# A hybrid mLSTM and windowed-attention layer on one core: an opening in smaller blocks, another order of the split products, and projection waits placed ahead of the attention matmuls

## The reference: what is computed

```
mod = silu(c) @ w_ada + b_ada                        # shift, scale, gate; for c and for c_ctx
u = rmsnorm(x, norm_pre_w) * (1 + scale) + shift
aq, ak, av, az, mq, mk, mv, mo, mz, mg, ga, gb = split(u @ w_in)     # w_in is 2048 x 11792
y_b = windowed_attention(rope(aq), rope(ak), av, cached context k, v, sink) * silu(az)
y_a = head_norm(mlstm forward + backward) * sigmoid(mo) * silu(mz)   # 4 heads x 256
merged = sigmoid(ga) * (y_a @ w_proj_a) + sigmoid(gb) * (y_b @ w_proj_b)
out = x + gate * rmsnorm(merged @ w_out, norm_post_w)
```

## Time and profile before

| | |
|---|---|
| median of 3 runs | 2206.77 us (2204.64 to 2209.23) |
| the profiled execution | 2208.73 us, its span 2206.9 us |
| TensorE (PE) matmuls busy | 2114.0 us, 96% of the span |
| VectorE (DVE) busy | 868.7 us, 39% |
| ScalarE (ACT) busy | 643.5 us, 29% |
| GpSimd (POOL) busy | 109.3 us, 5% |
| moved by DMA | 274.07 MB, 124 GB/s on average |
| granted TensorE clock, mean | 0.983 of full |

### The profile page before, as it was taken

How to read it: one execution, slowest core, us unless ns; L and a number is a source line. 1 busy time by engine, 2 the same in 40 slices (tenths; PEclk the granted TensorE clock), 3 DMA queues, 4 the chain that set the end, 5 groups by cost and what they waited for, 6 DMA issues and landing times.

```text
span 2206.9 us, 33978 instructions
## 1 busy us (share of the span) xinstructions
PE 2114.0 (96%) x13450; PEld 1968.9 (89%) x13450; DVE 868.7 (39%) x1674; ACT 643.5 (29%) x1046; POOL 109.3 (5%) x188
## 2 busy tenths in 40 slices
PE   2889999989999999999999989999999999999997
PEld 0559999989999999999999979999999999997885
DVE  4774755532223222323322224343434533352223
ACT  4764112133223232322322221313131422231221
POOL 2001000000000000000000000000000100000001
PEclk7999999999999999999999989999999999999998
DMA  6874755552234224222422243525252644323223
GB/s 243 276 239 124 210 170 174 157 152 83 76 86 117 76 83 120 86 76 76 120 78 81 85 117 81 160 79 152 86 154 81 199 124 120 118 88 124 77 77 143
DMA packets 295170, 274.07 MB, mean 124 GB/s; under 512 B 17920, under 2 KB 243960, under 8 KB 292640
## 3 DMA queue, kind: packets, MB, share of 16 engines
q1 hardware_dynamic: 282416, 218.21, 35.1%
q0 software_dynamic: 12656, 54.40, 6.7%
HBM read 232.65 MB, written 39.92 MB: 124 GB/s over the span
## 4 chain that ended last, share of the span: by engine, by line
PE 91%; DVE 3%; DMA 2%; ACT 1%; issue 1%; SPq 1%; DVEq 0%; POOL 0%; ACTq 0%; POOLq 0%
PE bank L1414 66%; PE bank L1629 10%; PE bank L1503 2%; PE bank L1329 2%; PE bank L1385 2%; PE bank L1368 2%; PE bank L1552 2%; PE bank L1543 1%; PE bank L1554 1%; PE bank L1476 1%; DMA Y<-in_x_prompt_dram 1%; DMA RAW<-in_w_in_dram 1%; DVE WL L875 0%; DVE XL L875 0%; DVE Y L917 0%
## 5 line engine op out<-in xcount | busy, mean ns | idle before, releaser
L1414 PE MATMUL bank<-XH,WH 128*128 128x320 f32 x3392 | 789.0, 314 | 7.1 <-issue 3.7
L1414 PE MATMUL bank<-XH,WL 128*128 128x320 f32 x3392 | 774.2, 310 | 0.0
L1414 PE MATMUL bank<-XL,WH 128*128 128x320 f32 x3392 | 773.9, 309 | 0.0
L857 DVE TENSOR_TENSOR WL<-RAW,WH 128x1024 fp32r<-128x1024 f32 x244 | 298.8, 1224 | 991.2 <-ACT WH L620 990.6
L620 ACT ACTIVATE WH<-RAW 128x1024 fp32r<-128x1024 f32 x244 | 258.3, 1059 | 1170.9 <-PE bank L1414 1013.7
L1414 PEld LDWEIGHTS bank<-XH,WH 128*128 128x128 f32 x3392 | 565.8, 188 | 16.0 <-issue 6.8
L1414 PEld LDWEIGHTS bank<-XL,WH 128*128 128x128 f32 x3392 | 568.1, 188 | 0.0
L1414 PEld LDWEIGHTS bank<-XH,WL 128*128 128x128 f32 x3392 | 567.8, 188 | 0.0
L1629 PE MATMUL bank<-WH,XH 128*128 128x512 f32 x320 | 128.6, 402 | 3.4 <-DVE WL L857 2.5
L1629 PE MATMUL bank<-WL,XH 128*128 128x512 f32 x320 | 125.3, 391 | 0.0
L1629 PE MATMUL bank<-WH,XL 128*128 128x512 f32 x320 | 125.2, 391 | 0.0
(11 more groups left out here) (196 smaller groups left out, 1504.4 us busy)
## 6 DMA issues: line engine op xcount, KB each, us to landing
RAW<-in_w_in_dram SPq DMA_DIRECT2D x180, 512.0 KB, 4.9
proj_dram<-OUTS POOLq DMA_DIRECT2D x92, 320.0 KB, 3.9
WORK<-in_w_ada_dram SPq DMA_DIRECT2D x54, 512.0 KB, 4.2
RAW<-in_w_ada_dram SPq DMA_DIRECT2D x42, 512.0 KB, 4.9
RAW<-in_w_out_dram SPq DMA_DIRECT2D x32, 512.0 KB, 3.9
WORK<-proj_dram SPq DMA_DIRECT2D x20, 640.0 KB, 5.0
WORK<-proj_dram POOLq DMA_DIRECT2D x32, 320.0 KB, 4.9
RAW<-in_w_proj_a_dram SPq DMA_DIRECT2D x16, 512.0 KB, 4.0
```

The costliest lines, as they stand in the source:

```text
L857: V.tensor_tensor(WL[:, gs % 2, :], RAW[:, gs % 4, :], WH[:, gs % 2, :].bitcast(F32), ALU.subtract).then_inc(lo_done, 1)
L1414: ins = pe.matmul(banks[n][:, 0:HALF_TOK], w[:, k, :], x[:, k0 + k, n * HALF_TOK:(n + 1) * HALF_TOK], start=(first and k == 0 and wi == 0) ...
```

## The change

There are four edits, quoted here from the diff, cut to the core.

The opening's loads and squares. Each block of x has its own semaphore, and its load stands behind that of one weight block. ScalarE squares block g right behind the high part of weight block g. VectorE does the mean at g = 6 and normalises one block ahead of each low part at g = 8 to 12:

```
-            for g in range(4):
-                start_load(g)
             for b in range(5):
+                start_load(b)
                 src = x_sample[0, b * P:(b + 1) * P, :] if b < NB else x_prompt[0]
-                sp.dma_start(XT[:, b, :], src).then_inc(x_in, 16)
-            for g in range(4, N_START):
+                sp.dma_start(XT[:, b, :], src).then_inc(x_in[b], 16)
+            for g in range(5, N_START):
                 start_load(g)
...
                 start_hi_part(g)
+                if g < 5:
+                    act.wait_ge(x_in[g], 16)
+                    if g:
+                        act.wait_ge(sq_done, g)
+                    nc.scalar.activation(SQ, XT[:, g, :], ACT.Square, accum_out=SS[:, g:g + 1]).then_inc(sq_done, 1)
...
-                if g == 4:
+                if g == 6:
                     dve.wait_ge(sq_done, 5)
                     V.tensor_scalar(SS[:, :], SS[:, :], 1.0 / D, EPS, ALU.mult, ALU.add).then_inc(ms_done, 1)
-                if g == 5:
+                if 8 <= g < 13:
                     dve.wait_ge(rstd_done, 1)
-                    for b in range(5):
-                        V.tensor_scalar(XT[:, b, :], XT[:, b, :], RSTD[:, b:b + 1], None, ALU.mult).then_inc(xn_done, 1)
+                    b = g - 8
+                    V.tensor_scalar(XT[:, b, :], XT[:, b, :], RSTD[:, b:b + 1], None, ALU.mult).then_inc(xn_done, 1)
```

```
+START_PE = []
+for _g, (_kind, _j, _q) in enumerate(START):
+    if _kind == "tiles":
+        START_PE += [(_g, 0), (_g, 1)]
+    elif _q == 0 and _g and START[_g - 1][0] == "tiles":
+        START_PE.insert(len(START_PE) - 1, (_g, None))
+    else:
+        START_PE.append((_g, None))
...
+def start_u(k):
+
+    c, i = divmod(k, 4)
+    return start_at("ada", 2 * c + 2, 4 + 2 * i) if i < 2 else start_at("ada", 2 * c + 3, 2 * i - 4)
...
-                    act.wait_ge(u_lo, 4 * c)
+                    act.wait_ge(u_lo, 4 * c - 3 + min(f, 3))
...
-                        if c < 3 and g == start_at("ada", 2 * c + 2, 4 + i):
+                        if c < 3 and g == start_u(4 * c + i):
                             modulate(c, i)
...
-                    if g == start_at("ada", 2 * (k // 4) + 2, 4 + k % 4) + 1:
+                    if g == start_u(k) + 1:
                         split_u(k)
...
-                    if j % 2 and 2 <= q < 7:
-                        transposed_x(j // 2, q - 2)
+                    if j % 2 and q >= 3:
+                        transposed_x(j // 2, q - 3)
```

The order of the products in a half tile and in the merge. The 32 matmuls with the high weights come first and wait only for `hi_done`; then a wait for `lo_done`, and the 16 with the low weights:

```
+            def split_products(banks, wslot, k0, done, first, last, k_wait=None):
...
                 for k in range(8):
                     if k_wait is not None:
                         pe.wait_ge(k_wait, k0 + k + 1)
-                    for wi, (w, x) in enumerate(((wh, XH), (wh, XL), (wl, XH))):
+                    for wi, x in enumerate((XH, XL)):
                         for n in range(2):
...
+                pe.wait_ge(lo_done, done)
+                for k in range(8):
+                    for n in range(2):
+                        ins = pe.matmul(banks[n][:, 0:HALF_TOK], wl[:, k, :],
+                                        XH[:, k0 + k, n * HALF_TOK:(n + 1) * HALF_TOK],
+                                        start=False, stop=(last and k == 7))
```

The waits in stages L1 and L2. `half` falls into `half_ready`, which holds the waits for `out_ready` and `hi_done`, and `half_products`. In the steps of attention and mLSTM the first now stands ahead of the step's other matmuls, the second stays behind them:

```
                 for s in range(2 * L1_TILES):
+                    t, x = divmod(s, 2)
+                    half_ready(2 * L1_TILES * kv, L1_TILES * kv, T_L1 + t, x)
                     if s == 2:
                         prepare()
...
                     if s % 2 == 0 and s >= 4:
                         probs_transposed((s - 4) // 2)
-                    t, x = divmod(s, 2)
-                    half(2 * L1_TILES * kv, L1_TILES * kv, T_L1 + t, x)
+                    half_products(2 * L1_TILES * kv, T_L1 + t, x)
```

More of the change, by code:

```diff
@@ L54, in start_at @@
     return START.index((kind, j, q))
+START_PE = []
[6 more added lines that the diff above has]
+        START_PE.append((_g, None))
+START_DONE = {}
+for _g, _part in START_PE:
+    if _part != 0:
+        START_DONE[_g] = len(START_DONE) + 1
 def start_w(g):
@@ L266, in hybrid_layer @@
         XT = OR
-        rows_in, const_in, x_in, aconst_in = sem("rows_in"), sem("const_in"), sem("x_in"), sem("aconst_in")
+        rows_in, const_in, x_in, aconst_in = sem("rows_in"), sem("const_in"), [sem(f"x_in{b}") for b in range(5)], sem("aconst_in")
         m0_in, mnull = sem("m0_in"), sem("mnull")
@@ L1370, in mod_piece, with start_tiles @@
                 ins.then_inc(start_used, 1)
-            def start_tiles(g, m):
+            def start_tiles(g, m, k):
                 pe.wait_ge(start_lo, g + 1)
                 wh, wl = start_wh[start_w(g)], start_wl[start_w(g)]
-                for k in range(2):
-                    kt = 2 * m + k
-                    if m == 5 and k == 1:
-                        mod_columns(7)
-                    pe.wait_ge(u_lo, kt + 1)
-                    for i in range(3):
-                        cs = slice(384 * k + P * i, 384 * k + P * i + P)
-                        for wi, (w, x) in enumerate(((wh, XH), (wh, XL), (wl, XH))):
-                            for n in range(2):
-                                ins = pe.matmul(bank[2 * i + n][:, 0:HALF_TOK], w[:, cs],
-                                                x[:, kt, n * HALF_TOK:(n + 1) * HALF_TOK],
-                                                start=(kt == 0 and wi == 0), stop=(kt == KT - 1 and wi == 2))
-                        if kt == KT - 1:
-                            ins.then_inc(tiles_done, 1)
-                if kt < KT - 1:
+                kt = 2 * m + k
+                if m == 5 and k == 1:
+                    mod_columns(7)
+                pe.wait_ge(u_lo, kt + 1)
+                for i in range(3):
+                    cs = slice(384 * k + P * i, 384 * k + P * i + P)
+                    for wi, (w, x) in enumerate(((wh, XH), (wh, XL), (wl, XH))):
+                        for n in range(2):
+                            ins = pe.matmul(bank[2 * i + n][:, 0:HALF_TOK], w[:, cs],
+                                            x[:, kt, n * HALF_TOK:(n + 1) * HALF_TOK],
+                                            start=(kt == 0 and wi == 0), stop=(kt == KT - 1 and wi == 2))
+                    if kt == KT - 1:
+                        ins.then_inc(tiles_done, 1)
+                if k == 1 and kt < KT - 1:
                     ins.then_inc(start_used, 1)
             pe.wait_ge(cs_done, 1)
-            for g in range(N_START):
+            for g, part in START_PE:
                 kind, j, q = START[g]
@@ L1399, in _, with product @@
                         mod_columns(j - 1)
-                    if j % 2 and 2 <= q < 7:
-                        transposed_x(j // 2, q - 2)
-                else:
-                    start_tiles(g, j)
-            def product(banks, wslot, k0, kk, first, last, k_wait=None):
+                    if j % 2 and q >= 3:
+                        transposed_x(j // 2, q - 3)
+                else:
+                    start_tiles(g, j, part)
+            def product(banks, wslot, k0, done, first, last, k_wait=None):
+                pe.wait_ge(hi_done, done)
+                return split_products(banks, wslot, k0, done, first, last, k_wait)
+            def split_products(banks, wslot, k0, done, first, last, k_wait=None):
                 wh = WH[:, wslot, :].rearrange("p (k n) -> p k n", k=8)
@@ L1411, in product, with half_ready @@
                         pe.wait_ge(k_wait, k0 + k + 1)
-                    for wi, (w, x) in enumerate(((wh, XH), (wh, XL), (wl, XH))):
+                    for wi, x in enumerate((XH, XL)):
                         for n in range(2):
-                            ins = pe.matmul(banks[n][:, 0:HALF_TOK], w[:, k, :],
-                                            x[:, k0 + k, n * HALF_TOK:(n + 1) * HALF_TOK],
-                                            start=(first and k == 0 and wi == 0), stop=(last and k == 7 and wi == 2))
+                            pe.matmul(banks[n][:, 0:HALF_TOK], wh[:, k, :],
+                                      x[:, k0 + k, n * HALF_TOK:(n + 1) * HALF_TOK],
+                                      start=(first and k == 0 and wi == 0), stop=False)
+                pe.wait_ge(lo_done, done)
+                for k in range(8):
+                    for n in range(2):
+                        ins = pe.matmul(banks[n][:, 0:HALF_TOK], wl[:, k, :],
+                                        XH[:, k0 + k, n * HALF_TOK:(n + 1) * HALF_TOK],
+                                        start=False, stop=(last and k == 7))
                 return ins
-            def half(i2, i, t, x, k_wait=None):
+            def half_ready(i2, i, t, x):
                 if x == 0:
@@ L1598, in _ @@
                         ins.then_inc(ml_ht, 1)
-                    t, x = divmod(s, 2)
-                    half(2 * L2_TILES * h, L2_TILES * h, T_L2 + t, x)
+                    half_products(2 * L2_TILES * h, T_L2 + t, x)
```

34 lines of the change are left out of this document (17 added, 17 removed).

## The result

The changed kernel takes 2191.89 us, the median of 4 runs (2190.65 to 2193.86), beside 2207.66 us for the kernel before in 4 runs. The ratio is 0.9931, 95% interval 0.9914 to 0.9948: the medians lie 15.8 us apart, and the interval is 11 to 19 us. The forecast was 2193.5, 13.2 less than before. The profiled execution took 2190.65 us for a span of 2188.9, so 18.0 less than the span before.

What follows compares the result with a forecast made beforehand. TensorE was taken as the bound, with holes in the opening; 9.3 + 3.7 = 13.0 us there and 0.15 from one hole, other terms 0, took the median from 2206.8 to 2193.5 us, range 2179 to 2204.

Steps and rivals of the forecast that it cites:

- 1. x: Opening, loads, squares and norm of x: low part of g = 12 ends at 47.7, 9.3 us earlier.
- rival C: The stretch after the opening's start gives most of the gain back: 3 to 8 us stay, 2202 us; 14%.
- 2. Blocks: Opening's three first "tiles" blocks: moving two splits behind the block saves 1.25 us each, 3.75 us in all.
- 0 between a first and a second block: Opening, from a first to a second block: TensorE itself is the limit, so no gain.
- halving 0 to 0.7, I take 0: Opening: halving a block frees a weight slot earlier, worth 0 to 0.7 us each, counted as 0.
- 3. The order of the products: Half tiles: new product order with a wait in the middle costs 0, between 0 and 0.2 us each.
- Rival D: The wait in the middle of each half tile breaks the stream, 0.2 us each, 49 us, 2242 us; 10%.
- The hole of the earlier trace: At 1750.69 us in the kernel before: a hole of 0.15 us, forecast to go.
- 4. The waits: Half-tile waits moved ahead of the attention: 0 taken, between 0 and -8.0 us over 40 steps.
- rival B: The waits cost the 0.2 us in 40 attention steps: 8 us more gain, 2185.5 us; 10%.
- Rival A: Smaller opening blocks keep TensorE busy throughout, so all idle time after 57 us goes: some 24 us, 2183; 18%.
- The chances: Whole kernel against the one before: faster 0.78, same 0.11, slower 0.11; 4.4 us can be told from no change.

Runs made afterwards that it cites:

- opening_only: The changed kernel with the product order and the waits of the kernel before, keeping the new opening; 2191.85 us, ratio 0.9933 to the kernel before.
- x_only: The kernel before with only the new loads, squares and norm of x, transposes one piece later; blocks whole, four splits together; 2195.10 us, ratio 0.9956.
- whole_blocks: The changed kernel with the w_in blocks multiplied whole, splits still two ahead and two behind; 2188.32 us, ratio 0.9924 to the kernel before.
- waits_only: The kernel before with only the half tile's waits moved ahead of the step's attention and mLSTM matmuls; 2207.80 us, ratio 1.0005.
- scores_first: The changed kernel with the 64-row scores matmuls put ahead of attend's 128-row ones in odd steps; 2194.59 us, ratio 0.9944 to the kernel before.
- norm_by_block2: As norm_by_block, but with GpSimd's filling of the gate sums behind its small loads instead of ahead; 2186.28 us, ratio 0.9916 to the kernel before.
- norm_by_block: As memset_early, plus a mean, power and normalisation for each block of x behind its own square; 2188.62 us, ratio 0.9918 to the kernel before.
- memset_early: The changed kernel with GpSimd's filling of the gate sums as its first work and squares in other scratch; 2190.32 us, ratio 0.9927 to the kernel before.

## Why the prediction was right, step by step

**The time.** 13.2 us were forecast and 15.8 measured (14.6 in opening_only). The number came near in part by luck: inside the opening a gain was missed and a loss was missed, and they largely cancel. The terms one by one, by the starts of L0:

**1. x: right.** The low part of g = 12 was to end at 47.7 and ends at 46.59 + 1.2 = 47.8. Its steps held one by one: mean at 30.0 (29.71), first normalisation at 31.9 (32.10). The length of the norm came out near, 9.6 us for the five where five times 1.75 is 8.8, for a reason that the prediction had not seen: four normalisations take 1.26 to 1.27, and the first 4.51. The group of five in the earlier trace rows hid this in its mean. In the kernel before, the first took 3.99 of the 8.77, beside the same filling of 3.50 us. x_only brings L0 10.7 us earlier and not 9.3, so the stretch behind gave some 1.4 more, little above what one start is good for; nothing was given back (rival C, false).

**2. Blocks: 4.8 us, forecast 3.75, and made otherwise.** The idle time that the move takes ahead of a first block was sized at 1.25, and that was right: from the scale to the block it is 1.27 less in each of the three in whole_blocks, and in the changed kernel 9.41 (93.87 to 103.28) where it was 10.66 (105.71 to 116.37). The step "0 between a first and a second block" failed: the first blocks then run at full clock (6.77 to 5.54 us for the first of them in whole_blocks), and the stretches that hold them shrink by 3.0 us in all. A further 0.4 lies ahead of the first scale. I had read "TensorE itself is the limit" in the earlier trace rows, where 36 matmuls take 6.75 and 6.89 in the first blocks and 5.53 in a second; that the difference was clock, and that a shorter pause ahead of the block could return it, could be asked of the same trace and I left it out. The step "halving 0 to 0.7, I take 0" failed in its sign: it costs 2.5, since the block's slot comes free a piece later. The gain expected from freeing a slot earlier came from looking at the half that stands first, but the count goes up only behind the second, which now has a piece ahead of it. 7.3 - 2.5 = 4.8, and 10.7 + 4.8 = 15.5. The runs are less sharp than this: between x_only and opening_only, in one group, the medians differ by 3.25 and the ratios by 5.1 us, so the sum of the term, 3.75, is not refuted; what failed is how it was made up.

**3. The order of the products: 0, right to within its interval.** Rival D is false: 7.04 us per half tile with one wait in the middle or with eight. The hole of the earlier trace rows is gone from the chain; 0.15 us is too little for any median to show. At the entry to L1 the half tile starts 1.25 earlier as expected (idle 2.02), and the idle time ahead of `prepare` was to be 2.96 and is 4.12. What was not forecast is the granted clock behind it. TensorE's timeline and the windows over `prepare` and over the half tiles ahead of it:

```profile
430.22 0.56 PE L1436 MATMUL bank<-XH,WH 128*128 128x320 f32 x2 [2.02 <-ACT WH L639]
...
448.67 5.24 PE L1494 MATMUL bank<-WORK 128*128 128x512 f32 x6 [4.12 <-DMA WORK<-in_attn_sink_dram]
```

```profile
430.22:444.55 14.33, 14.33 (x96) 14.07 (x96) 3.66 (x3) 4.06 (x5) 0.96 (x3) 1.00 0.66 180
448.67:453.91 5.24, 5.24 (x7) 1.92 (x8) 1.23 (x1) 4.12 (x5) 0.39 (x1) 0.53 0.90 244
```

`prepare` runs at 0.53, near the lower of the two levels (1.2 GHz), and takes 5.24 us where 2.84 stood. The half tiles ahead of it gain: 14.33 us for 96 matmuls, where the chain before took 15.88 from 446.97 to 462.85 with a slow beginning. From the end of L0 to the end of `prepare` it is 25.7 us after and 23.7 before, a loss of 2.0. By 656.78, `prepare` of the next group, the changed kernel is 14.8 us ahead (671.58 before), so 1.3 of the 2.0 are back by then; from which places was not settled, and no median shows either.

**4. The waits: 0, right.** waits_only is level, and the half tile behind the scores keeps its 0.2 us with the wait gone from ahead of it, so rival B is false. That the change of rows holds the load of the weights back was argued only before; scores_first moves 0.2 us by moving the 64-row matmuls, which shows the place and not yet the mechanism. The rule quoted there from the Trainium skill ("TensorE: Matmul & The Clock Gate", Part 2, step 1), that weight loads are pulled ahead of running matmuls when the row groups don't conflict or when they go to the background buffer, is not contradicted by this: the 0.2 us follows the change of rows and not the wait.

**Rival A** is false: a full turn still holds 4.6 us of idle time, and the window from 57.00 to 79.16, which now takes in the first block, 22.16 - 18.90 = 3.3.

**The chances.** By their own rule they add to 0.79, 0.10 and 0.11 and not to 0.78, 0.11 and 0.11; nothing hangs on it.

## What to carry to other kernels

When an engine waits for a chain of small steps on other engines, price what the pause does to the granted clock of the work behind it, not the pause alone: here a first block took 7.07 us behind the longer pause and 5.55 behind the shorter. Of these 1.5 us 1.1 reached the next block, nearly as much as the 1.3 us of pause that were removed. Before a piece of work is halved so that something else can go between, look at which event returns its buffer: if it is the end of the second half, the buffer comes back later, not earlier. And split a group's mean into its single rows: one outlier in five (4.51 beside 1.26) named a collision that could be moved away. Moving it paid only in part by itself (L0 0.4 us earlier), and with the norm taken block by block and the small loads left where they were, it paid 6.3.

## What the runs showed of the hardware

- Filling 128x4096 floats on GpSimd (3.5 us) holds VectorE's work beside it: a normalisation takes 4.51 us instead of 1.26 to 1.29. When the filling stands at 6.10 to 9.6, two small casts on VectorE take 3.26 us where they took 0.26, as these two rows of VectorE's timeline show, first of norm_by_block2, then of the changed kernel:

```profile
6.42 3.26 DVE L884 CAST CS<-VC 128x16 fp32r<-128x16 f32 x2
```

```profile
6.46 0.26 DVE L884 CAST CS<-VC 128x16 fp32r<-128x16 f32 x2
```

- It seems to go the other way too: the power of one column on GpSimd takes 0.56 us with VectorE idle (12.85 above) and 1.52 beside a normalisation that begins 0.16 earlier; this was seen in the four later ones of norm_by_block2 and again of norm_by_block, and not tried apart.
- In memset_early the first square of x begins at 11.99 and the last at 28.05, against 10.22 and 25.59. The small loads of the gate biases and the state on GpSimd's queue ran from 6.10 on, beside the loads of x, and not from 3.12. With the loads at 3.11 and the filling at 6.10 the last square is at 25.67. Loads and filling changed places together, so that the small loads did it is likely and not shown.
